# Norms in two halves of tokens, two norms merged, and rotation angles between copies

## What is computed

```python
def first_block(x, ...):
    h = modulate(rms_norm(x, ffn1_norm), sh1, sc1)
    x = x + 0.5 * g1 * swiglu(h, gate1, up1, down1)
    h = modulate(rms_norm(x, mix_norm), sh2, sc2)
    u_f, q_lat, kv_lat, k_rope, gate_logits = split(h @ w_in)
    y_a = fourier_mix(u_f) @ w_fourier_out
    y_b = mla_attention(q_lat, kv_lat, k_rope, positions, ...) @ w_mla_out
    x = x + g2 * ((gate_a * y_a + gate_b * y_b) @ w_out)
    h = modulate(rms_norm(x, ffn2_norm), sh3, sc3)
    x = x + 0.5 * g3 * swiglu(h, gate2, up2, down2)
    return rms_norm(x, final_norm)

def second_block(x, ...):
    h = rms_norm(x, g_pre_mix) * (1 + sc1) + sh1
    proj = h @ w_in_2
    o = concat(nsa_attention(rope(...), ...), dsa_attention(rope(...), ...)) @ w_out_2
    x = x + gt1 * rms_norm(o, g_post_mix)
    h = rms_norm(x, g_pre_ffn) * (1 + sc2) + sh2
    return x + gt2 * rms_norm(square(relu(h @ w_up)) @ w_down, g_post_ffn)
```

## Time and profile before

| | us |
|---|---|
| median of 3 runs | 2074.18 (2074.07 to 2074.76) |
| profiled execution, its own time | 2074.3 |
| its span | 2072.5 |
| granted TensorE clock, mean | 0.966 |
| PE busy | 1936.2 (93%) |
| DVE busy | 1212.3 (58%) |
| POOL busy | 1150.9 (56%) |
| ACT busy | 363.2 (18%) |

### The profile page before, as it was taken

How to read it: one execution, slowest core, us unless ns; L and a number is a source line. 1 busy time by engine, 2 the same in 40 slices (tenths; PEclk the granted TensorE clock), 3 DMA queues, 4 the chain that set the end, 5 groups by cost and what they waited for, 6 DMA issues and landing times.

```text
span 2072.5 us, 25215 instructions
## 1 busy us (share of the span) xinstructions
PE 1936.2 (93%) x8980; PEld 1526.7 (74%) x8980; DVE 1212.3 (58%) x1822; ACT 363.2 (18%) x749; POOL 1150.9 (56%) x1075
## 2 busy tenths in 40 slices
PE   6999999989899999899999978985999979999997
PEld 3788888868657888788888847664666748788785
DVE  7888478746644124887078355675774367405713
ACT  2100000022145111200000031112555230000001
POOL 3577777756440667576777643575000338767861
PEclk8999999999999999999999989896999989999998
DMA  8654555422220234454355221233000112233231
GB/s 277 203 175 158 189 167 183 151 85 89 64 62 1 62 102 140 129 189 132 118 191 172 89 68 41 81 72 93 1 1 1 41 41 87 95 101 94 89 101 40
DMA packets 231130, 216.51 MB, mean 104 GB/s; under 512 B 20305, under 2 KB 227342, under 8 KB 231054
## 3 DMA queue, kind: packets, MB, share of 16 engines
q1 hardware_dynamic: 230000, 214.84, 32.7%
q10 hardware_dynamic: 1054, 0.66, 0.1%
...
## 4 chain that ended last, share of the span: by engine, by line
PE 86%; DVE 10%; ACT 1%; issue 1%; POOL 1%; DMA 0%; ACTq 0%; DVEq 0%; POOLq 0%; SPq 0%
PE ps L614 24%; PE ps L616 24%; PE ps L615 23%; PE ps L891 5%; PE ps L914 4%; PE ps L900 3%; DVE rb L1437 1%; PE ps L660 1%; DVE tt L1931 1%; DVE tt L1654 1%; DVE xT L1932 1%; DVE ada_sum L1466 1%; DVE score L1815 1%; PE ps L645 1%; PE ps L851 0%
## 5 line engine op out<-in xcount | busy, mean ns | idle before, releaser
L525 POOL TENSOR_TENSOR w_lo<-raw,w_hi 128x512 fp32r<-128x512 f32 (+2 forms) x612 | 798.7, 1335 | 12.8
L614 PE MATMUL ps<-h_hi,w_hi 128*128 128x512 f32 x1424 | 565.6, 397 | 28.1 <-DVE h_lo L1459 26.7
L615 PE MATMUL ps<-h_lo,w_hi 128*128 128x512 f32 x1424 | 557.7, 392 | 0.0
L616 PE MATMUL ps<-h_hi,w_lo 128*128 128x512 f32 x1424 | 557.6, 392 | 0.0
L518 POOL TENSOR_TENSOR w_hi<-raw,ones 128x8 fp32r<-128x8 f32 x153 | 34.6, 226 | 870.1 <-PE ps L616 820.5
L614 PEld LDWEIGHTS ps<-h_hi,w_hi 128*128 128x128 f32 x1424 | 269.5, 189 | 92.0 <-issue 35.1
L1466 DVE SCALAR_TENSOR_TENSOR ada_sum<-ada,cT,ada_sum 128x256 f32<-128x256 f32 x378 | 325.1, 860 | 13.4
L615 PEld LDWEIGHTS ps<-h_lo,w_hi 128*128 128x128 f32 x1424 | 269.5, 189 | 58.0 <-issue 2.4
L616 PEld LDWEIGHTS ps<-h_hi,w_lo 128*128 128x128 f32 x1424 | 269.1, 189 | 57.8
L614 PE MATMUL ps<-g_hi,w_hi 128*128 128x512 f32 x608 | 237.4, 390 | 3.1 <-ACT sg L1396 3.1
L616 PE MATMUL ps<-g_hi,w_lo 128*128 128x512 f32 x608 | 236.7, 389 | 0.0
...
## 6 DMA issues: line engine op xcount, KB each, us to landing
...
```

What stands on the lines that cost most here:

```text
L525: last = pool.tensor_tensor(lo[:, c], src[:, c], hi[:, c].bitcast(F32), ALU.subtract)
L614: pe.matmul(o, wh, xh, start=start, stop=False)
L615: pe.matmul(o, wh, xl, start=False, stop=False)
L616: return pe.matmul(o, wl, xh, start=False, stop=stop)
```

## The change

Every norm but the first runs in two halves of 256 tokens. The last pair of output groups ahead of a norm is computed for tokens 0 to 255 first, then for the others (last_pair); between the second half's groups stands the first half's sum over features (half_sum). The first two weight tiles behind the norm are taken together, half A for both, then half B for both (first_tiles), and the sum of half B stands in the middle of the first tile's half A. DVE and ACT follow with halves: boundary, half_inverse (L1659), half_scaled (L1674), half_low (L1682), half_high, half_root. The first tile of each of the four products behind a norm (EXTRA) has a weight buffer of its own, we_hi and we_lo, and its split waits only for tile_used of n-3.

Norms 3 and 4 become one: the sum weighs the squares by gain2 (the final gain squared plus EPS), and the final gain goes into the factor A_PREMIX. Block 1's own output, which block 2's residual needs, gets a sum of its own on PE (y_sum), a root, a reciprocal (block1_root) and eight multiplications (block1_out) among block 2's rotations. rotate2(0) to (3) go between the natural chunks. The angles of block 1 are cut into three parts, with two branch copies behind the first and two behind the second. POST2 and PRE3 run in halves with PE's mid_sum, and the end (POST3) in halves with output DMAs of half the rows and twice the columns.

The core of the diff:

```diff
+EXTRA = (W_MIX, W_FFN2, W_IN2, W_FFN3)
+    we_hi = place("we_hi", [P, SLOT], F32R, at=at(20))
+    we_lo = place("we_lo", [P, SLOT], F32R, at=at(52))
...
-            if not first:
+            if per:
                 pool.wait_ge(tile_used, i * per + (n - 1))
+            elif n in EXTRA:
+                pool.wait_ge(tile_used, n - 3)
+            elif not first:
+                pool.wait_ge(tile_used, last_user(n) + 1)
...
+        def last_pair(i, tiles, kc, xh, xl, ready=lambda u: None):
+            for u, n in enumerate(tiles):
+                pe.wait_ge(split_done, n + 1)
+                ready(u)
+                for m in range(2):
+                    last = part(ps[:, 2 + m, HALF[0]], n, kc, m, xh, xl, kc * u, HALF[0], u == 0, n == tiles[-1])
+                    if n == tiles[-1]:
+                        last.then_inc(half_mm, 1)
+            for u, n in enumerate(tiles):
+                for m in range(2):
+                    last = part(ps[:, 6 + m, HALF[1]], n, kc, m, xh, xl, kc * u, HALF[1], u == 0, n == tiles[-1])
...
+                    if u == 0 and m == len(tiles) - 1:
+                        half_sum(i, 0)
...
+        def first_tiles(n0, banks, a0, b0, between, after=lambda: None, first_done=None):
+            for h in range(2):
+                t = HALF[h]
+                for u in range(2):
+                    n = n0 + u
+                    pe.wait_ge(split_done, n + 1)
...
+                    for k in range(NC):
+                        pe.wait_ge((lo_a, h_lo_done)[h], (a0, b0)[h] + k + 1)
...
+                        if h == 0 and u == 0 and k == 3:
+                            between()
...
+        def boundary(i, add, factor, shift, a0, b0):
+            for m in range(ON_DVE, NC):
+                add(m, 0)
+                if m == ON_DVE:
+                    norm_add(i, ON_DVE - 1)
+            half_inverse(i, 0)
+            half_scaled(0, 0, factor, a0)
+            add(ON_DVE, 1)
+            for m in range(1, NC + 1):
+                if m < NC:
+                    half_scaled(m, 0, factor, a0)
+                half_low(m - 1, 0, shift, a0)
+                if m == 2:
+                    add(ON_DVE + 1, 1)
+                if m == 6:
+                    half_inverse(i, 1)
+            for m in range(NC + 1):
+                if m < NC:
+                    half_scaled(m, 1, factor, b0)
+                if m:
+                    half_low(m - 1, 1, shift, b0)
...
-        norm_inverse(3)
+        step(dve.tensor_tensor(fac[:, A_PREMIX:A_PREMIX + 8], fac[:, A_PREMIX:A_PREMIX + 8], vec[:, V_FINAL:V_FINAL + 8], ALU.mult))
+        boundary(N_PRE2, lambda m, h: add_half(N_PRE2, m, h, W_IN2 - 1, column(fac, A_G3 + m)), A_PREMIX, 72, 16, 24)
...
-        chunks_then_add(4, final_norm)
-        norm_inverse(4)
-        modulated(3, A_PREMIX, 72)
...
+        block1_root()
         for i in range(4):
             rotate2(4 + i, qn[:, i])
+            block1_out(i)
             select(2)
```

More of the change, by code:

```diff
@@ L538, in _ @@
                     split(1, NC, 256, first=True)
-                with pool.Fori(1 if n0 == 0 else 0, iters) as it:
+                elif n0 == W_FFN2:
+                    for u in range(4):
+                        split(n0 + u, NC, 256)
+                with pool.Fori({0: 1, W_FFN2: 2}.get(n0, 0), iters) as it:
                     for u in range(2):
@@ L546, in _ @@
             n0 = W_FFN3 + 16 * half
-            with pool.Fori(0, 4) as it:
+            if half == 0:
+                for u in range(4):
+                    split(n0 + u, NC, 256)
+            with pool.Fori(2 - 2 * half, 4) as it:
                 for u in range(2):
@@ L639, in norm_sum @@
         def norm_sum(i):
-            if i:
-                pe.wait_ge(n_std, i)
-            if i in DIRECT:
-                for m in range(NC):
-                    pe.wait_ge(n_sq, 8 * i + m + 1)
-                    last = pe.matmul(ps[:, B_NORM], ones[:], sq[:, m % 2], start=m == 0, stop=m == NC - 1)
-                    last.then_inc(n_acc if m < NC - 1 else n_sum, 1)
-                return
             pe.wait_ge(n_acc, last_added(i))
@@ new lines, in mid_sum, with part @@
+        def mid_sum(h):
+            t = HALF[h]
+            for m in range(NC):
+                pe.wait_ge(mid_sq, NC * h + m + 1)
+                last = pe.matmul(ps[:, B_ADA, t], ones[:], sq[:, m % 2, t], start=m == 0, stop=m == NC - 1)
+                last.then_inc(mid_acc if m < NC - 1 else (sum_a, n_sum)[h], 1)
+        def part(o, n, kc, m, xh, xl, k0, t, start, stop):
+            wh, wl = slot(w_hi, n, kc, 256), slot(w_lo, n, kc, 256)
+            c = slice(P * m, P * m + P)
+            for k in range(kc):
+                last = mm3(o, wh[:, k, c], wl[:, k, c], xh[:, k0 + k, t], xl[:, k0 + k, t],
+                           start and k == 0, stop and k == kc - 1)
+            return last
@@ L748, in run_ffn @@
                 pe.wait_ge(mod_read, (4, 5, 7, 7)[2 * i + half])
-                first = i == 0 and half == 0
-                if first:
-                    gate_up(0, 0, 0, tiles=(1,))
-                with pe.Fori(int(first), iters) as it:
+                if half == 0:
+                    if i == 0:
+                        gate_up(0, 0, 0, tiles=(1,))
+                    else:
+                        first_tiles(n0, (0, 1, 2, 3), 8, 16, lambda: half_sum(N_FFN2, 1))
+                        for u in range(2):
+                            ada_mm_step(s0 + u)
+                with pe.Fori(1 - half, iters) as it:
                     gate_up(i, half, it)
@@ L1007, in next_tile @@
             pe.wait_ge(split_done, n + 1)
-        n = W_IN2
-        next_tile(n)
         pe.wait_ge(rp_raw, 9)
-        signal(pair_of_groups((1, 0), n, 24, rp_mm), rp_mm, 1, 2)
-        rot(9, R64, P, rp_raw2)
-        pend[0], r[0] = 1, 2
-        n = W_IN2 + 1
-        next_tile(n)
-        for c in range(2):
-            proj(n, c)
-        flush()
+        first_tiles(W_IN2, (1, 0, 4, 7), 16, 24, lambda: half_sum(N_PRE2, 1), first_done=rp_mm)
+        pe.matmul(ps[:, B_NORM], ones[:], sq_sum[:], start=True, stop=False)
+        for m in range(ON_DVE, NC):
+            last = pe.matmul(ps[:, B_NORM], ones[:], sq[:, m % 2], start=False, stop=m == NC - 1)
+        last.then_inc(y_sum, 1)
+        r[0] = 4
         next_tile(W_IN2 + 3)
@@ L1113, in _ @@
         pe.wait_ge(o_lo_done, 12)
-        for i in range(8):
+        for i in range(6):
             n = W_OUT2 + i // 2
@@ L1159, in norm_squares @@
+    def norm_squares(act, i, ready, first, src, chunks=range(NC)):
+        for m in chunks:
             act.wait_ge(ready, first + m + 1)
```

491 lines of the change are left out of this document (356 added, 135 removed).

## The result

The changed kernel took 2084.92 us (median of 20 runs, 2079.61 to 2091.44), the kernel before 2074.84 in the runs beside it: a ratio of 1.0042, with a 95% interval of 1.0032 to 1.0053. It is slower by 0.4%, where 2070.7 was forecast and 2051 to 2081 was the range. The profiled execution took 2085.4, with a span of 2083.5 against 2072.5. Runs of both kernels spread: of the 20 of before, 13 lie between 2073.9 and 2076.0, six between 2079.5 and 2081.5 and one at 4975.1, and the profiled one (2074.3) is of the first group, while the profiled one of after lies at its median.

A forecast was written before the change was run, and what follows sets the result against it. PE was taken to bound the kernel, a stream of matmuls that stops at each norm. Terms -4.4 - 4.6 - 4.7 + 5.9 + 2.3 + 9.1 = +3.6 won, from 2074.3 to 2070.7 us, range 2051 to 2081.

The forecast's parts named there:

- Angles (9.1 won): Block 1's Fourier projection: copies of ya no longer wait for all angles, 6.7 idle and 2.4 at half clock go.
- MIX (4.4 lost): Last output pair to second weight tile at the mix norm: 52.3 us in halves against 47.9 before.
- My layout: MIX in halves laid out by hand: 44.9 us with DVE undisturbed, 49.5 with POOL's contention, against 47.9 before.
- FFN2 (4.6 lost): Stretch at FFN2's norm: 46.9 us in halves with contention plus 2 for the clock, 48.9 against 44.3 before.
- POST2 with PRE3 (4.7 lost): Post-mix norm and the norm behind it: 66.9 us against 62.2, two whole-chunk sums becoming four over halves.
- PRE2 (13.3 won, 7.4 given back): Block 2's two norms merged: 61.0 us against 74.3; behind them, rotations and block 1's output give 7.4 back.
- the 61.0 of the sum: PRE2's forecast stretch: 51.8 plus 1.5 for the clock, a 4.3 wait for POOL's split and 3.4 for rotations' products.
- 3.4, 4.8 and 2.6 of the sum: PRE2: 3.4 for rotations' products, 4.8 for rotate2(2) and (3) behind the last natural chunk, 2.6 for block1_out.
- End (2.3 won): Kernel's end: 44.4 us against 46.7, no POOL work left, second half's tail under the first's transposes.
- My bounds: PE's half clock behind a norm: costs 2.0 us now, in the change 0 to 3.8 at MIX and FFN2.
- The rival "slower": Full contention and the clock falling twice at every norm: 5.8 lost, 2080.1 us, chance 0.20.
- the signs I had named: Profile after: DVE half instructions' means near 0.9 us, PE's h_lo waits more and shorter (1 to 2 us).

The follow-up runs named there:

- experiment 1: Kernel before with only the change's angles in three parts between the branch copies: 2068.94 us, ratio 0.9958 to the kernel before.
- experiment 10: Changed kernel with whole norms, two buffers, unread matmuls in PE's idle time at norms, last ada step back behind the fourth pair: 2054.26 us, ratio 0.9886 to before.
- experiment 9: Changed kernel with the last two ada steps moved between half A and half B of the last pair: 2088.34 us, ratio 1.0055 to before.
- experiment 12: Changed kernel, ada steps between halves, last pair's tiles in turn, third split held back except FFN2, unread matmuls at POST2 and W_FFN3: 2070.01 us, ratio 0.9967 to before.
- experiments 4: Changed kernel with all norms whole again, merged norm, third buffer and angles in three parts kept: 2069.3 us, ratio 0.996 to before.
- experiment 5: Changed kernel with all norms whole and the third weight buffer taken away too: 2064.45 us, ratio 0.9932 to before.
- experiment 2: Changed kernel with POOL's split of the third tile held back until the norm's last h_lo is done: 2078.28 us, ratio 0.9996 to before.
- experiment 7: Changed kernel, halves and extra buffer kept, plus unread matmuls in PE's idle time at its norms: 2081.14 us, ratio 1.0014 to before.
- experiment 6: Changed kernel with whole norms and two buffers, plus unread matmuls in PE's idle time at the norms: 2057.05 us, ratio 0.9896 to before.
- experiment 11: Kernel before, nothing of the change, plus unread matmuls in PE's idle time at its norms: 2078.82 us, ratio 1.0008 to before.

## Why the prediction was wrong

**Angles (9.1 won): right**, 9.8, shown by experiment 1.

**MIX (4.4 lost): right in size, 4.5, by luck.** My layout had the halves win 3.0 (44.9 for 47.9), contention take 4.6 of it back, 2 for the clock at the norm and 0.8 for the ada wait. Holding the third split back gives only 1.2; whole norms with two buffers still lose 4.3, and experiment 10 takes 3.8 of its MIX by moving the ada steps alone. So in whole norms 3.8 belongs to the moved ada steps, sized at 0.8 since I priced the wait and not the fall of the clock behind it. In the change itself that part isn't separable: experiment 9 took the ada wait away and a wait for POOL came in its place. The 3.0 of the layout shows in no run: in experiment 12, whose last pair has another order, MIX loses 4.3 without contention.

**FFN2 (4.6 lost): near**, 3.5, of which experiments 4 and 5 give 1.9 to the third buffer alone, and experiment 2 gives 2.0 to contention.

The net of the terms was missed by 14.4: 6.3 at PRE2 (5.9 won was forecast, 0.4 lost measured), 6.0 at POST2, 3.2 at the end and 0.6 at the start, less 1.8 at the angles and FFN2.

**POST2 with PRE3 (4.7 lost): the first step that failed**, 10.7. I priced contention by the chunk on DVE alone. There it was too high (means of 0.62 and 0.58, not 0.9, and none ahead of W_FFN3). What cost was who stands behind it: PE's two waits of 3.20 and 4.40 for half B's squares ahead of half A's mid sums. Experiment 2 gives 5.0 to contention, experiment 7 gives 3.9 to the clock; the two overlap, since both act on the same waits. The order in the queues is read from the traces: no run here changes it.

**PRE2 (13.3 won, 7.4 given back): the second.** The win up to the natural chunks was 11.8 (13.0 less 1.2), and that it came so near is luck: the 61.0 of the sum held 3.4 for the rotations' products, which in the kernel stand behind the first natural product. Without them 16.7 was forecast, 4.9 too much, with a wait of 3.22 for POOL inside the last pair that the sum lacked. The part given back was 12.3 from there on (11.4 from the table's mark): 3.4, 4.8 and 2.6 of the sum are 10.8 of it. It is 10.2 from that mark in experiment 5, so it belongs to the merged norm and its rotations, not to the halves. A part that the sum lacked is the clock behind the next rotation, where PE waits 4.53 for 2.80: 0.56 from 1370 to 1375, while before stays at 1.00.

**End (2.3 won): the third**, 0.9 lost, against 1.1 won whole. "The second half's tail lies under the first's transposes" failed: the transposes of half A stand behind half B's sum on PE, and this waits 4.07 for DVE, which does all of half A's residual first. To it comes the wait of 2.43 for POOL inside the last pair.

**The clock.** My bounds were right at whole norms (2.0 a norm: experiment 6 gets 1.2 to 2.3 at each), but it also fell at places where I had looked for none, behind the ada wait (0.55) and behind a rotation's (0.56). **The rival "slower"** (2080.1) had contention and a clock that falls more often, and came nearest; it had neither POOL's late second tile nor the order in the queues of POST2 and the end. By its own terms it would have come to about 2077.7: 51.8 + 3.1 + 4.3 + 3.4 is 62.6, so PRE2 wins 4.3 net and not 1.9. Of the signs I had named, h_lo in more and shorter waits held in number and not in sum, and the means of 0.9 held only while POOL ran (0.62 and 0.58 over all). The Trainium skill, *SBUF — State Buffer*, section "Who interferes with whom", gives the rule by which a DVE instruction with two SBUF inputs and a GpSimd one that reads SBUF block each other; the rows of MIX and POST2 agree (0.48 alone, 1.1 to 1.5 beside w_lo).

What is left open: the 1.6 that halves cost at FFN2 beyond the buffer, where the halves lose at MIX without contention, the 5.2 that experiment 11 loses between the natural chunks and POST2, how waits and clock share POST2, and what another order of DVE's copies there and at the end would give.
